# A decoder trunk on one core: the three products of every weight tile, regrouped into a pass with the high operand and a pass with the low operand

## The reference, cut to what matters

```python
def swiglu(h, w_gate, w_up, w_down):
    return (jax.nn.silu(h @ w_gate) * (h @ w_up)) @ w_down

def layer(x, st_h, st_conv, st_gla, reset_first, p):
    h = rmsnorm(x, p['norm_pre'][0])
    x = x + 0.5 * rmsnorm(swiglu(h, p['w_ffn_gate'][0], ...), p['norm_post'][0])
    h = rmsnorm(x, p['norm_pre'][1])
    m, h_last, new_conv, S_fin = mixer(h, st_h, st_conv, st_gla, reset_first, p)
    x = x + rmsnorm(m, p['norm_post'][1])
    h = rmsnorm(x, p['norm_pre'][2])
    x = x + 0.5 * rmsnorm(swiglu(h, p['w_ffn_gate'][1], ...), p['norm_post'][2])
    return x, h_last, new_conv, S_fin
```

## Time and profile before

| | |
|---|---|
| median of 3 runs | 2124.01 us (2123.99 to 2124.31) |
| the profiled execution's own time | 2123.84 us |
| its span, first to last instruction | 2121.8 us |
| PE busy, of the span | 2112.5 us |
| DVE / ACT / POOL busy | 1442.3 / 1291.8 / 710.0 us |
| mean DMA rate | 165 GB/s |

### The profile page before, as it was taken

How to read it: one execution, slowest core, us unless ns; L and a number is a source line. 1 busy time by engine, 2 the same in 40 slices (tenths; PEclk the granted TensorE clock), 3 DMA queues, 4 the chain that set the end, 5 groups by cost and what they waited for, 6 DMA issues and landing times.

```text
span 2121.8 us, 41190 instructions
## 1 busy us (share of the span) xinstructions
PE 2112.5 (100%) x17197; PEld 2087.8 (98%) x17197; DVE 1442.3 (68%) x1902; ACT 1291.8 (61%) x1989; POOL 710.0 (33%) x708
## 2 busy tenths in 40 slices
PE   9999999999999999999999999999999999999999
PEld 9999999999999999999999999999999999999998
DVE  7555857778986658845584558577689867576454
ACT  8544657658786657653564456576587765575444
POOL 3112512525654225511250124124275533152112
PEclk9999999999999999999999999999999999999999
DMA  7555555445554565555555555554465544655553
GB/s 259 168 166 164 169 180 157 150 144 175 170 159 140 151 186 164 169 168 165 167 168 168 167 164 167 179 159 142 143 191 158 155 146 152 183 167 169 166 172 129
DMA packets 100552, 350.98 MB, mean 165 GB/s; under 512 B 11409, under 2 KB 12305, under 8 KB 100369
## 3 DMA queue, kind: packets, MB, share of 16 engines
q1 hardware_dynamic: 99936, 347.68, 53.7%
q10 hardware_dynamic: 432, 0.68, 0.1%
HBM read 343.45 MB, written 4.87 MB: 164 GB/s over the span
## 4 chain that ended last, share of the span: by engine, by line
PE 96%; DVE 1%; POOL 1%; issue 1%; DMA 0%; ACT 0%; SPq 0%; DVEq 0%; POOLq 0%; ACTq 0%
PE psD L519 91%; PE psM L612 1%; POOL ssum L1652 1%; PE psM L519 0%; DVE val L1508 0%; PE psM L653 0%; PE psM L725 0%; DVE ring L1183 0%; DMA raw_ring<-in_w_gu 0%; PE psM L688 0%; POOL hidden_pair L1853 0%; PE psS L539 0%; PE psM L732 0%; PE psD L505 0%; PE psM L592 0%
## 5 line engine op out<-in xcount | busy, mean ns | idle before, releaser
L519 PE MATMUL psD<-operand,ring 128*128 128x288 f32 x10992 | 1461.1, 294 | 1.0 <-DVE operand L1251 1.0
L519 PEld LDWEIGHTS psD<-operand,ring 128*128 128x128 f32 x10992 | 1442.9, 188 | 8.7 <-issue 3.7
L1183 DVE TENSOR_TENSOR ring<-raw_ring,ring 128x1024 fp32r<-128x1024 f32 (+2 forms) x656 | 824.3, 1257 | 107.8 <-ACT ring L839 107.2
L839 ACT ACTIVATE ring<-raw_ring 128x1024 fp32r<-128x1024 f32 (+2 forms) x656 | 671.9, 1027 | 94.1 <-DMA raw_ring<-in_w_gu 47.1
L519 PE MATMUL psD<-hidden_pair,ring 128*128 128x288 f32 x4224 | 564.0, 294 | 0.9 <-POOL hidden_pair L1853 0.9
L519 PEld LDWEIGHTS psD<-hidden_pair,ring 128*128 128x128 f32 x4224 | 555.0, 188 | 5.4 <-POOL hidden_pair L1853 4.1
L1853 POOL TENSOR_TENSOR hidden_pair<-hid,hidden_pair 128x288 fp32r<-128x288 f32 x176 | 214.3, 1217 | 876.1 <-ACT hidden_pair L1127 876.1
L1127 ACT ACTIVATE hidden_pair<-hid 128x288 fp32r<-128x288 f32 x176 | 77.9, 443 | 241.2 <-DVE hid L1189 241.1
L1652 POOL TENSOR_TENSOR ssum<-ssum,sq 128x288 f32<-128x288 f32 x145 | 166.2, 1146 | 157.5 <-ACT sq L853 154.5
L1123 ACT ACTIVATE act<-gate 128x288 f32<-128x288 f32 x176 | 78.3, 445 | 225.7 <-DVE gate L1189 225.1
L1189 DVE TENSOR_TENSOR hid<-psD,act 128x288 f32<-128x288 f32 x174 | 79.1, 455 | 190.0 <-PE psD L519 183.0
(11 more groups left out here) (240 smaller groups left out, 1206.6 us busy)
## 6 DMA issues: line engine op xcount, KB each, us to landing
raw_ring<-in_w_gu SPq DMA_DIRECT2D x351, 512.0 KB, 3.6
raw_ring<-in_w_d SPq DMA_DIRECT2D x128, 448.0 KB, 3.3
raw_ring<-in_w_in SPq DMA_DIRECT2D x80, 512.0 KB, 3.6
raw_ring<-in_w_d SPq DMA_DIRECT2D x64, 512.0 KB, 3.6
raw_ring<-in_w_out SPq DMA_DIRECT2D x32, 512.0 KB, 3.6
x<-in_xT SPq DMA_DIRECT2D x8, 288.0 KB, 6.9
gates<-in_w_ax SPq DMA_DIRECT2D x4, 512.0 KB, 4.5
S<-in_st_gla SPq DMA_DIRECT2D x4, 512.0 KB, 4.6
```

The lines of the kernel that those rows point to most:

```text
L519: mm = e.matmul(out, w[:, kt * P:(kt + 1) * P], t[:, kt, :], start=(kt == 0 and part == 0), stop=(kt == KT - 1 and part == 2))
L839: e.activation(wh[u % RING][:, part], raw[u % RING][:, part], ACT.Copy).then_inc(hi_ready, 1)
L1183: e.tensor_tensor(wl[u % RING][:, part], raw[u % RING][:, part], wh[u % RING][:, part].bitcast(F32), ALU.subtract).then_inc(lo_ready, 1)
```

## The change

In the general loop of `unit`, the one loop over row tiles becomes two. The first makes the two products with the high operand, (wh, high) and (wl, high), for each row tile. The second makes the product (wh, low) for each. The waits are divided in the same way: the first loop waits for the high part of a tile (`hidh_ready`, `hh_ready`, `mix_hh`), the second for its low part. Units 1 to 3 keep their order. Unit 0 goes through the changed loop. The number of matmuls, their shapes, tiles and PSUM banks stay as they are.

```diff
                 if u == 0 and kt == KT // 2:
                     e.wait_ge(lo_ready, 1)
                 if hidden is not None:
+                    e.wait_ge(hidh_ready, hidden + kt + 1)
+                if operands is not None:
+                    e.wait_ge(operands[0], operands[2] + kt + 1)
+                for w in (w_h, w_l):
+                    e.matmul(out, w[:, kt * P:(kt + 1) * P], xh[:, kt, :], start=(kt == 0 and w is w_h), stop=False)
+            for kt in range(KT):
+                if hidden is not None:
                     e.wait_ge(hidl_ready, hidden + kt + 1)
                 if operands is not None:
-                    e.wait_ge(operands[0], operands[1] + kt + 1)
-                for part, (w, t) in enumerate([(w_h, xh), (w_h, xl), (w_l, xh)]):
-                    mm = e.matmul(out, w[:, kt * P:(kt + 1) * P], t[:, kt, :],
-                                  start=(kt == 0 and part == 0), stop=(kt == KT - 1 and part == 2))
+                    e.wait_ge(operands[1], operands[2] + kt + 1)
+                mm = e.matmul(out, w_h[:, kt * P:(kt + 1) * P], xl[:, kt, :], start=False, stop=(kt == KT - 1))
             mm.then_inc(unit_done, 1)
...
                 if k == 0 and s.kind == "wout":
-                    need = (mix_hl, 8 * s.mixer)
+                    need = (mix_hh, mix_hl, 8 * s.mixer)
                 elif k == 0 and s.c == 0:
-                    need = (hl_ready[g], operand_round(s) - DT)
+                    need = (hh_ready[g], hl_ready[g], operand_round(s) - DT)
```

## The result

The changed kernel takes 2142.3 us (median of 4 runs, 2140.8 to 2143.8), the kernel before 2124.0: a ratio of 1.0087, 95% interval 1.007 to 1.0105. The change makes the kernel slower by 18 us. The profiled execution took 2143.62 us, 19.8 more than the profiled one of before. One run of a kernel further down (`unit0_old`, 2285.7 us at a mean clock of 0.851) ran slow from end to end and is left out of its median.

A forecast was written before the change was run, and what follows sets the result against it. PE was taken as the bound, through the spacing of 15,216 matmuls. The terms -3.1 - 0.3 + 0 + 0 = -3.4 us took the profiled 2123.84 to 2120.4, forecast as 2120.6 us at the median; range 2109 to 2148.

The forecast's parts named there:

- Part 1: PE's waits for POOL's low part of the last hidden tile: 14 vanish, 3.1 us, two shrink, 0.3 us.
- Part 2: Waits for normed inputs, in unit 0 at the start: 0 gain, bounds -0.2 to +0.2 us; unit 1 still starts near 10.9.
- Part 3: Some 330 more waits on PE's queue, covered by the queue ahead of the array: 0; if not, 7 us lost.
- Part 4: Spacing of matmuls in the general loop under the new order: 0 change, bounds -9 to +27 us.
- the present mixture: General loop's matmuls, about half at each of 129.9 and 131.2 ns, mean about 130.5; taken to stay unchanged.
- the two rates: General loop before the change: 129.9 and 131.2 ns a matmul at the same clock, read as order not mainly setting the rate.
- The nearest row: Units 2 and 3 at the start, an order alike in kind: 24 matmuls in 3.17 and 3.18 us, 132.3 ns each.
- The bound: Matmul spacing in the general loop: 129.9 ns or a little less below, 132.3 ns above.
- The slow rhythm of units 2 and 3: Rival, chance 0.24: a stream of pairs costs 132.3 ns wherever it runs, in every unit; 27 us more, 2148 us.

The follow-up runs named there:

- `unit0_old`: The changed kernel with unit 0 alone put back in the order of before: 2141.1 us, against 2142.3 for the changed kernel.
- the exchanged order: Kernel before with (wh, low) and (wl, high) exchanged in its one loop per row tile: 2118.65 us with old waits, 2115.09 with divided waits.
- 48 bytes: Weight ring begun 48 bytes into its area instead of 112, in both kernels: kernel before 2156.3 us, changed kernel 2138.1 us.
- alternating rows: Kernel before, old waits; even row tiles make (wh, high), (wl, high), (wh, low), odd ones (wh, low), (wl, high), (wh, high): 2153.9 us.
- `after_lead24`: The changed kernel with the weight ring 16 bytes below its place, 96 bytes ahead of it instead of 112: 2159.4 us.
- `three_passes`: Against the kernel before, each product in its own pass, (wh, high), (wh, low), (wl, high), low-part waits in the first pass: 2189.5 us, one run.

## Why the prediction was wrong

**Part 1, the hidden tile: right.** Predicted 3.4 us. The waits went as forecast, in 14 of 16 places entirely and in two down to 0.2 us, where I had left 0.44 each. The gain with nothing else changed is 2118.65 - 2115.09 = 3.6 us in the exchanged order, or 3.1 by the runs of before beside each. For the changed kernel's own order the step had a blind side: it compared the new order and new waits with the old, and not with the new order and the old waits, where 22 us were at stake. That did no harm to the sum, since the change has both.

**Part 2, the start: too narrow.** I counted 0 within 0.2 us; it was 2.4 us in the profiled run, and by its time one more of the four runs had it too. That unit 1 waits for its high part "whatever unit 0 does" held only for the landing seen in one execution of before. With the second half tile landing at 8.23 us, where ACT had taken it up at 6.93 before, unit 0 itself sets the start, and sixteen products are then left to make instead of twelve, some of them at the lower clock.

**Part 3, more waits on PE's queue: right.** The divided waits in the exchanged order cost nothing that can be seen. (They are 304 in the changed kernel and not 330: a new normed input meets 8 gate units, and not 12. The loop also has 72 matmuls more than the 15,216 counted, 0.1 us at 1.8 ns each. Neither moves the sum.)

**Part 4, the rhythm: the step that failed.** "I take 0 change, the present mixture: the two rates show that one order can run at either, so that the order is not what mainly sets it". The second reason was the full DMA load beside units 2 and 3. Both reasons were wrong. Units 1 to 3's order takes 132.3 ns without that load; and two rates 1.3 ns apart within an order say nothing about a third rate in another. The nearest row gave 132.3 ns and 132.2 was measured. The bound was right and the choice within it was not: by the nearest row the sum would have been 2148, 6 us too high instead of 22 too low. The 6 us are the size of the step's rise, 1.8 ns in that sum against 1.4 to 1.6.

The Trainium skill ("TensorE: Matmul & The Clock Gate", section "Back-to-back issue gap") gives a matmul's spacing as a function of its column count and the clock, with no term for the order. Taken to mean that the order costs nothing, it isn't borne out: with the same two instructions 15,200 times over, the step went from 129.9 to 133.4 ns with order and place alone.

**The rivals.** The slow rhythm of units 2 and 3 is what happened, at 0.24. Its mechanism as I put it, a stream of pairs costs 132.3 ns "wherever it runs", is half of the truth: at another place of the weights the row order costs as much. The range of 2109 to 2148 us held the result only because it was drawn wide enough for this rival; the forecast itself had the sign wrong.

## What to carry to other kernels

Where PE never idles, a change in the order of its matmuls must first be priced by the distance between starts, counted in windows; here some 1.5 ns a step were worth five times all waits that the change removed or more. To give a late operand more slack, exchange products within the row tile and divide the waits; at this place of the weights, leaving the stream's period alone was what kept the rate. And an order that was tuned together with the place of its tiles isn't comparable with another order until that one has had its own places tried: the verdict on this change turns round at 48 bytes.

## What the runs showed of the hardware that was not expected

- The distance between starts of the same LDWEIGHTS and MATMUL pairs (128x128 by 128x288, clock 1.00) lay between 129.9 and 133.4 ns, depending on the order of the products and on where the weights begin, to within 16 bytes; taking away the 28 words ahead of them moved the kernel before by 23 us.
- At this place (112 bytes), streams with a period of three products (the old order, the exchanged one, and the one with the low product a row tile late) ran at 130 to 131 ns; streams of two passes, three passes, or alternating rows at 132 or more.
- The old order held a rate by repeating six distances that add up to 780 ns, or to 786 or 787; which of the two, stretch by stretch, was not explained.
- After 2.2 us without a matmul, PE went on at the lower clock, and the mean clock was still 0.56 in the window from 10.6 to 13.5 us. It cost 2.4 us together with the late landing. In `after_lead24` one wait of 1.2 us left the clock at 1.00; in `three_passes` it fell after two waits, of 0.9 and 1.2 us.
